# Forgetting-attention value products issued in groups of four key tiles instead of two

## The reference, cut to what matters

```python
def fox_block(qp, q, c):
    s = jnp.einsum('bqhd,bkhd->bhqk', q.astype(f32), kf) * SCALE
    s = s + jnp.swapaxes(c, 1, 2)[..., :, None] - ck[:, :, None, :]
    s = jnp.where(kpos[None, :] <= qp[:, None], s, NEG_INF)
    p = jax.nn.softmax(s, axis=-1)
    return jnp.einsum('bhqk,bkhd->bqhd', p, vf)
```

## Time and profile before

| | |
|---|---|
| median of 3 runs | 2607.64 us (2605.27 to 2612.8) |
| the profiled execution, its own time | 2605.0 us |
| its span, first to last instruction | 2603.2 us |
| TensorE busy | 2478.4 us, 95% of the span |
| VectorE busy | 1374.3 us, 53% |
| ScalarE busy | 942.9 us, 36% |
| Pool busy | 386.0 us, 15% |
| value products of forgetting pairs (line 2111) | 640 records, 145.9 us |
| value products of differential pairs (line 2108) | 320 records, 147.1 us |

### The profile page before, as it was taken

The page is one execution under the profiler, slowest core; times in us unless marked ns, Lnnn a source line. Parts: engine busy times, 40 slices in busy tenths (PEclk is TensorE's granted clock), DMA queues, the critical chain, the costliest instruction groups (busy, mean ns, idle before and its releaser), DMA issues.

```text
span 2603.2 us, 35097 instructions
## 1 busy us (share of the span) xinstructions
PE 2478.4 (95%) x13569; PEld 1977.2 (76%) x13569; DVE 1374.3 (53%) x2227; ACT 942.9 (36%) x1869; POOL 386.0 (15%) x398
## 2 busy tenths in 40 slices
PE   7999999999999999999988899899899989999998
PEld 5788888789999999999855565565565556888897
DVE  5311123315443333542368888788788786655553
ACT  4123331112222222111136645654664666322221
POOL 0100001121100000112352113103212242000000
PEclk9999999999999999999989999999999999999999
DMA  5688888958987666888560523235054023544432
GB/s 153 161 223 207 202 210 206 209 138 243 244 237 226 207 215 181 233 206 175 145 158 9 126 50 89 55 77 130 5 131 107 28 83 108 181 133 130 143 118 89
DMA packets 583892, 388.65 MB, mean 149 GB/s; under 512 B 318672, under 2 KB 538776, under 8 KB 577416
## 3 DMA queue, kind: packets, MB, share of 16 engines
q1 hardware_dynamic: 574592, 367.80, 53.8%
q0 software_dynamic: 9136, 18.63, 2.1%
HBM read 284.83 MB, written 134.79 MB: 161 GB/s over the span
## 4 chain that ended last, share of the span: by engine, by line
PE 75%; DVE 6%; SPq 5%; ACT 5%; issue 4%; DMA 3%; POOL 1%; DVEq 0%; ACTq 0%; POOLq 0%
PE p_acc L876 13%; PE p_acc L881 12%; PE p_acc L880 12%; PE a_op L2111 5%; PE a_sb L2086 4%; PE a_sb L2087 3%; PE a_op L2108 3%; PE a_sa L2064 2%; PE a_sa L2067 2%; PE e_U L1428 2%; PE e_U L1430 2%; PE e_U L1429 2%; ACT a_e L1924 2%; DVE a_nmax L1955 2%; PE a_sa L2065 2%
## 5 line engine op out<-in xcount | busy, mean ns | idle before, releaser
L876 PE MATMUL p_acc<-p_h_hi,p_w_hi 128*128 128x384 f32 (+1 forms) x1960 | 716.1, 365 | 11.9 <-DVE p_ev L586 5.5
L881 PE MATMUL p_acc<-p_h_hi,p_w_lo 128*128 128x384 f32 (+1 forms) x1920 | 688.0, 358 | 0.0
L880 PE MATMUL p_acc<-p_h_lo,p_w_hi 128*128 128x384 f32 (+1 forms) x1920 | 687.8, 358 | 0.0
L1955 DVE TENSOR_REDUCE a_nmax<-a_sa 128x1 f32<-128x1024 f32 (+7 forms) x384 | 347.2, 911 | 125.0 <-PE a_sa L2069 45.1
L1924 ACT ACTIVATE a_e<-a_sb 128x512 f32<-128x512 f32 (+3 forms) x640 | 310.4, 533 | 278.5 <-PE a_sb L2087 183.8
L876 PEld LDWEIGHTS p_acc<-p_h_hi,p_w_hi 128*128 128x128 f32 x1960 | 370.8, 189 | 52.7 <-issue 12.8
L881 PEld LDWEIGHTS p_acc<-p_h_hi,p_w_lo 128*128 128x128 f32 x1920 | 362.1, 189 | 30.4
L880 PEld LDWEIGHTS p_acc<-p_h_lo,p_w_hi 128*128 128x128 f32 x1920 | 362.6, 189 | 29.0
L692 DVE TENSOR_TENSOR p_w_lo<-p_raw,p_w_hi 128x1024 fp32r<-128x1024 f32 x96 | 125.6, 1308 | 368.8 <-ACT p_w_hi L619 368.7
L2086 PE MATMUL a_sb<-a_q,a_k 128*128 128x512 f32 (+2 forms) x640 | 276.5, 436 | 20.6 <-ACT a_e L1924 18.1
L2087 PE MATMUL a_sb<-a_q,a_k 68*128 68x512 f32 (+2 forms) x640 | 237.1, 374 | 0.0
(11 more groups left out here) (233 smaller groups left out, 3475.6 us busy)
## 6 DMA issues: line engine op xcount, KB each, us to landing
p_raw<-in_w_in SPq DMA_DIRECT2D x98, 512.0 KB, 5.7
s_k_raw<-scratch_kS SPq DMA_DIRECT2D x64, 512.0 KB, 6.9
scratch_kS<-in_cache_fox_k SPq DMA_DIRECT2D x32, 512.0 KB, 6.6
scratch_kS<-in_cache_diff_k SPq DMA_DIRECT2D x32, 512.0 KB, 6.4
s_v_raw<-in_cache_fox_v SPq DMA_DIRECT2D x8, 2048.0 KB, 11.0
s_v_raw<-in_cache_diff_v SPq DMA_DIRECT2D x8, 2048.0 KB, 10.0
a_q<-scratch_q_hi SPq DMA_DIRECT2D x32, 512.0 KB, 13.3
a_k<-scratch_k_hi SPq DMA_DIRECT2D x32, 512.0 KB, 15.2
```

What stands on the lines that cost most here:

```text
L876: nc.tensor.matmul(acc[a % 2][:, 0:n], hi, h_hi[p][:, k, at:at + n], start=(k == 0), stop=False)
L880: nc.tensor.matmul(acc[a % 2][:, 0:n], hi, h_lo[p][:, k, at:at + n], start=False, stop=False)
L881: last = nc.tensor.matmul(acc[a % 2][:, 0:n], lo, h_hi[p][:, k, at:at + n], start=False, stop=(k == DK - 1))
L1955: nc.vector.tensor_reduce(nmax[:, b % 2, c, col:col + 1], scores_of(ev[1]), axes, ALU.max, negate=True).then_inc(a_maxed, 1)
```

## The change

Forgetting products are issued in every fourth iteration (u = 4k+1), four at a time (x = u-5 to u-2), instead of in every odd one, two at a time. The condition on the differential pair is the same as before in effect: the four units all belong to one forgetting pair and one block, since all blocks have a multiple of 4 units. Differential products and all other steps stay where they are.

```diff
             if u >= 2 and is_diff(B_UNITS[u - 2][0]):
                 multiply(u - 2)
-            elif u >= 3 and u % 2:
-                multiply(u - 3)
-                multiply(u - 2)
+            elif u >= 5 and u % 4 == 1 and not is_diff(B_UNITS[u - 2][0]):
+                for x in range(u - 5, u - 1):
+                    multiply(x)
             for _ in share:
                 stages(1)
```

## The result

| | before | after |
|---|---|---|
| median of 6 runs each, same chip | 2606.68 us (2603.14 to 2612.97) | 2655.43 us (2643.44 to 2662.78) |
| ratio, 95% interval | | 1.0177 (1.0145 to 1.0209) |
| the profiled execution, its span | 2603.2 us | 2659.1 us |
| granted clock over the span | 0.984 | 0.968 |

The changed kernel is 48.8 us slower by the medians. The forecast was no change that can be told, 2609 with a range up to 2621, so it was wrong: "slower" had 0.25, and but for rival 3 (0.02) no case in it came near 2655. The runs after differ with the clock that they were granted: 2643.44 came with 0.973, 2662.78 with 0.964.

A forecast was written before the change was run, and what follows sets the result against it. TensorE, busy 95% of the span, was taken as the bound. Per pair 1.05 + 0.35 + 0 + 0.8 - 1.0 - 1.3 = -0.1; 2605.0 + 0.4 - 1.0 + 0.35 + 2 = 2606.8, as median 2609; range 2596 to 2621.

The forecast's parts named there:

- rival 3: ScalarE would wait for one of six slots of e; 1.8 us exposed 40 times, over 2670 us; chance 0.02.
- the clock: Half-clock stretches on TensorE with longer idle at places 19, 35 and 40: 2 us lost, bounds 5 gained to 14 lost.
- places 23 and 27: Iterations of a forgetting pair that lose their products: 0 at 23 (bounds gain 0.35, loss 1.3), gain 0.35 at 27.
- The price of a switch: On TensorE, going from 128-column matmuls to 64-column product pairs and back: 0.35 us per group, forty groups fewer.
- the ceiling of 14: Most that merging groups can give if TensorE never waits: 40 x 0.35 = 14.0 us, 0.54%.
- Places 7, 11, 15, 31: Iterations of a forgetting pair that lose their products: gain 0.35 us each at 7 and 11, 0 at 15 and 31.
- Place 35: Products between two "a" units covered a wait for an exponential: about 1.5 us idle uncovered, loss 1.3, switch included.
- Place 19: Products between two "a" units covered a wait for an exponential: about 1.0 us idle uncovered, loss taken as 1.0.
- Place 3: "a" units there wait for VectorE's maximum alone, and the 3.58 us group lets it catch up: gain 0.35 us.
- Place 39: Products move from ahead of a 1.87 us wait to ahead of a 1.58 us wait before "SUM": gain 0.8 us.
- The head: First product's 3.63 us wait for Pool's masks gets two iterations of scores ahead: gain 1.0 us, bounds 0 and 3.6.
- Rival 2: Products were cover: 2626 if places 19, 23, 27, 31, 35 each lose 1.3, 2621 by half clock at eight; chance 0.23.

The follow-up runs named there:

- the filled kernel: Changed kernel plus unread 256-column matmuls ahead of nearly every TensorE wait over 0.3 us in forgetting pairs: 2612.79 us, ratio to before 1.0013.
- kernel with the maxima first: Changed kernel with unread matmuls, running-sum additions of places 3, 4, 23, 24, 27, 28 put behind the "a" steps, unread matmuls of 5, 23, 25, 29 removed: 2615.25 us.
- the fours late: Changed kernel with products in twos for units 0 to 11 and in fours for units 12 to 39 of each forgetting pair: 2656.27 us, ratio 1.0176.

## Why the prediction was wrong, point by point

Two steps of the forecast failed: the clock, put at 2 us and measured at about 31, and the waits that the moved products had covered at places 23 and 27, put at a gain of 0.35 a pair and measured at a loss of 3.0. One reading at its start was off, without weight in the sum: rows 2 leave 12.3 to 12.8 us without TensorE work in three of the stretches and 19.5 in the first, not "10 to 12".

**The price of a switch** held: 0.35 was forecast per group. Singles in place of twos show 0.26 to 0.32, and places 7 and 11 gained 0.32 and 0.33. (In its working, twice 0.84 is 1.68 and not 1.70, and the first loss is 0.08; the total moves by 0.01.) The four units take the forecast 3.58 us, and the next score pass starts at once:

```profile
1818.63 3.65 PE L2111 MATMUL a_op<-a_e,a_v 128*64 128x512 f32 x16
1822.21 0.39 PE L2086 MATMUL a_sb<-a_q,a_k 128*128 128x256 f32 x1
```

Forty groups at this price are 12 to 13 us, so the ceiling of 14 was nearly right; no kernel tested it as a whole. The Trainium skill says on its page "TensorEngine Tiling (Array Packing)" (Key Properties) that a change of the tiling mode drains TensorE, but gives no time; the trace agrees in that each group costs 0.26 to 0.33 us for the way there and back. That it is a drain which takes this time, no run here shows.

**Places 7, 11, 15, 31** came out as forecast, within 0.16. **Place 35** did so for the stated reason. After rows 6 it now reads:

```profile
1906.06 0.34 PE L2065 MATMUL a_sa<-a_k,a_q 66*128 66x384 f32 x1
...
1907.85 0.50 PE L2064 MATMUL a_sa<-a_k,a_q 128*128 128x512 f32 x1 [1.45 <-ACT a_sa L1891]
...
1911.78 0.50 PE L2064 MATMUL a_sa<-a_k,a_q 128*128 128x512 f32 x1 [0.48 <-ACT a_sa L1891]
...
1912.90 3.65 PE L2111 MATMUL a_op<-a_e,a_v 128*64 128x512 f32 x16
```

The uncovered wait is 1.45 (forecast 1.5), and the following one stayed at 0.48 (0.47 in rows 6). The loss of 1.4 (forecast 1.3) is in the table. **Place 19** lost 1.0 as forecast, in the filled kernel; its uncovered wait was shorter than the 1.0 foreseen, 0.5 to 0.8.

**Places 23 and 27 failed.** They had been put at 0 and +0.35, the first "because no second "a" unit follows in the same iteration", and cost 1.4 and 1.6: 3.4 of the 4.7 us by which the sum of a pair (4.8 instead of 0.1) was off. The argument looked only at who waits within the same iteration. At place 27 the victim is the "b" unit of two places later, whose exponential stands on ScalarE behind X, and X behind a maximum of 1.22 us; the kernel that moves this one X got 1.8 us per pair back. The rivals' text had the condition in view ("when the exponential (L1891) ends later than the scores of the next place") but applied it to X, where what ended late was E behind X. At place 23 the "a" unit waits for an X whose maximum stands behind the addition of place 22: with this addition moved, the wait of 0.87 went. It gained nothing, since a wait of 1.68 came at place 25.

**Place 3** was expected to gain 0.35 and lost 0.27 with its segment: without the products, the "a" unit of place 5 is ready for its buffer before VectorE has done the addition and the maximum, 0.35 of wait. That "a group of 3.58 us lets it catch up" was true behind the group, not ahead of it. The kernel with the maxima first took this wait away, for 0.17 of the segment (8.86 instead of 9.03).

**Place 39** gained 0.53 instead of 0.8. The first wait grew (1.87 in rows 8, 2.41 now) and the one in front of the "SUM" matmuls did not fall under 0.5:

```profile
1924.79 0.80 PE L2064 MATMUL a_sa<-a_k,a_q 128*128 128x512 f32 x1 [2.41 <-ACT a_sa L1891]
...
1928.07 3.26 PE L2111 MATMUL a_op<-a_e,a_v 128*64 128x512 f32 x12
...
1932.26 1.08 PE L2136 MATMUL a_cT<-a_run,a_ones 128*64 128x512 f32 x4 [0.92 <-DVE a_gap L1969]
...
1931.03 0.75 DVE L2008 SCALAR_TENSOR_TENSOR a_w<-a_e,a_lam 128x512 f32<-128x512 f32 x1 [1.88 <-PE a_op L2111]
1931.69 0.42 DVE L2027 TENSOR_TENSOR a_run<-a_run,a_e 128x256 f32<-128x256 f32 x1
```

The forecast named this cost (W waits for the product of place 37 with the addition behind it) and then said that the product "ends about when VectorE gets there". It does not: VectorE stands idle for 1.88 us at W.

**The head.** The wait of 3.63 in rows 9 is gone, and 1.07 of it is back at place 5:

```profile
1339.34 1.01 PE L2067 MATMUL a_sa<-a_k,a_q 66*128 66x384 f32 x2 [1.07 <-DVE a_nmax L1955]
1340.41 3.55 PE L2111 MATMUL a_op<-a_e,a_v 128*64 128x512 f32 x12
```

But from place 0 to 6 of the first pair it takes 28.7 us, where it took 28.0. The half clock there lasts 23.9 us instead of 17.0, so the forecast gain of 1.0 did not come. How much of this is the change is not shown: in the other kernels it was 17.1 to 23.9 us with the four at the head, and 17.0 to 27.3 with twos.

**The clock** is the largest error: 2 us forecast, about 31 lost. The bounds were 5 gained and 14 lost, and both were built on wrong terms: only places 19 and 35 were thought to bring a half-clock stretch, of 3.4 us each as in rows 10. After the change there are three in each of the later two pairs, of 6.8, 10.2 and 6.8 us, and five of 3.4 to 10.2 us each in the first two (in the first, beside the one at its head). Place 19 has one of 10.2 in all four pairs; place 35 has none. The first stretch of pair 4 begins at place 16:

```profile
1833.12 0.50 PE L2086 MATMUL a_sb<-a_q,a_k 128*128 128x512 f32 x1 [0.77 <-ACT a_e L1924]
...
1834.54 0.62 PE L2086 MATMUL a_sb<-a_q,a_k 128*128 128x512 f32 x1 [0.20 <-ACT a_e L1924]
1834.96 0.63 PE L2087 MATMUL a_sb<-a_q,a_k 68*128 68x512 f32 x1
1835.39 0.63 PE L2086 MATMUL a_sb<-a_q,a_k 128*128 128x512 f32 x1
```

The scores of place 15 waited 0.77, much as before (0.76). Those of place 16 waited 0.20, without the products that used to stand between the two, and from 1834.8 passes that started every 0.24 start every 0.43. So place 15, costed at 0 and nearly right in waits, was not free in clock: pairs 2, 4 and 6 have this stretch, pair 0 has not. The DMA engines are as busy in it (share 0.92 in the row of 1834.80), but they don't bring it: with the fillers places 16 and 17 have shares of 0.88 to 0.95 at full clock, and with the fours late the clock of pair 0 fell to half at place 16 for 6.8 us with a share of 0.1. The second stretch begins at 1848.4 and still holds at place 21, where sixteen records of products take 4.91 instead of 3.65:

```profile
1849.70 0.69 PE L2064 MATMUL a_sa<-a_k,a_q 128*128 128x384 f32 x1 [0.53 <-ACT a_sa L1891]
...
1856.10 4.91 PE L2111 MATMUL a_op<-a_e,a_v 128*64 128x512 f32 x16
```

In these two stretches TensorE is busy for 6.80 of 6.80 and 9.28 of 10.20 us, so much of the slower clock goes into the time. At half clock a stretch costs at most half its length; against the filled kernel the segments with the three cost 2.8 of 3.4, 3.2 of 5.1 and 2.5 of 3.4 us.

That the half clock follows the waits is shown by the fillers: with them all half clock in pairs 2, 4 and 6 disappears, in both orders. Single waits were opened again in two kernels, and the clock shows there what one wait can do. With those at 23 (0.87) and 29 (1.43) unfilled, it fell at 29 in three of four pairs and never at 23; with one of 1.68 at place 25, it fell there in two of four. So one wait of 1.4 to 1.7 us is enough, but not each time, and the length alone does not decide: in pair 4 after the change the clock held through 1.43 at 29, 2.04 at 32 and 1.45 at 35, and fell behind 0.77 and 0.20 at 15 and 16. What decides is open.

The Trainium skill's page "TensorE: Matmul & The Clock Gate" (Part 1, What's actually happening) has the clock low by default and released by activity. By this rule the prediction had pointed to the upper of its bounds, 14; the runs agree with its direction and went to twice that size.

**The signs named beforehand** told the case only in part. Rival 2 was to hold if L2064's waits passed 15 or the granted clock fell below 0.9: the waits were 11.7 to 12.9 a stretch, and the clock 0.80 and 0.87 in the first two stretches, 0.91 in the others. Rival 2 was right as a mechanism, cover lost and half clock, but it had them as alternatives (2626 or 2621). They came together, and the clock part was larger than either. Its 18.6 us for the waits are near the 19 measured partly by luck: it charged 1.3 to place 31 as well, which lost 0.16, and gave place 3 a gain. Rival 3 did not happen: in the stretches read, E (L1924) waits for the scores (L2087) or, once, for VectorE (L2001), and not for a product.

## What to carry to other kernels

Before moving a block of matmuls, go beyond the wait of the same iteration: for every engine queue, write down what stands ahead of the instruction that TensorE waits for next, and ask whether the moved block used to cover it. When TensorE is nearly full but has many waits of 0.5 to 2 us, price a few more of them by the clock first: here it took 31 us where the waits themselves took 19. Unread matmuls in such waits (14 us of 2610 in the kernel before) can be worth more than a change of the order.

## What the runs showed of the hardware

- TensorE's clock fell to 1.2 GHz although it was busy for 86% of each forgetting stretch (135.50 of 156.70 us, 112.81 of 130.90) and, in pairs 2, 4 and 6, never idle for more than 0.9 us at a time in the 30 us before the fall at place 16. Longer waits in the same pair, up to 2.04 us, passed without a fall.
- More work in the waits was faster: 127 matmuls more per pair took 8.4 to 13.9 us off each pair in the changed order, 89 more took off 0.2 to 5.4 in the order before.
- Fillers in the head of the stage as well (57 more, where every kernel has 14 to 31 us at half clock) changed the time by nothing that can be measured (2594.04 against 2594.76 us).
- To go from 128-column fp32 score matmuls to pairs of 64 columns and back costs 0.26 to 0.33 us per group. Beside 128-column value matmuls (rows 5) no such cost was seen: a unit takes 0.84 us there, and one more unit in a group of 64-column pairs 0.855.
